# Cross attention: probabilities scaled by row before they are turned, and values as the stationary operand

## What is computed

```python
def memory_cross_attention(xn, memn, w_xq, w_xkv, w_xo):
    q = (xn @ w_xq).reshape(bsz, s, X_HEADS, X_HEAD_DIM)
    k, v = jnp.split(memn @ w_xkv, 2, axis=-1)
    scores = jnp.einsum("bshd,bmhd->bhsm", q, k) * (X_HEAD_DIM ** -0.5)
    p = jax.nn.softmax(scores, axis=-1)
    o = jnp.einsum("bhsm,bmhd->bshd", p, v).reshape(bsz, s, D_MODEL)
    return o @ w_xo
```

## Time and profile before

| what | value |
|---|---|
| median of 3 runs | 2702.12 us (2698.0 to 2704.2) |
| the profiled execution | 2703.93 us, its span 2702.2 us |
| mean granted TensorE clock | 0.984 |
| the attention block with the block of turns, from PE's first score to the first product with `w_xo`, layer 0 | 220.33 to 241.16 us |
| the same, layer 1 | 701.00 to 721.82 us |

### The profile page before, as it was taken

How to read it: one execution, slowest core, us unless ns; L and a number is a source line. 1 busy time by engine, 2 the same in 40 slices (tenths; PEclk the granted TensorE clock), 3 DMA queues, 4 the chain that set the end, 5 groups by cost and what they waited for, 6 DMA issues and landing times. The chain is left out here.

```text
span 2702.2 us, 79563 instructions
## 1 busy us (share of the span) xinstructions
PE 2553.2 (94%) x35795; PEld 2164.4 (80%) x35795; DVE 1013.4 (38%) x2465; ACT 446.6 (17%) x1027; POOL 162.0 (6%) x212
## 2 busy tenths in 40 slices
PE   8999999999979999999999999888999999999997
PEld 6888788788869989999989897666758678877775
DVE  4511444371120110110110101446673478765666
ACT  2101000110123322000000001410000445542000
POOL 0100000010012122000000000000000000001000
PEclk9999999999979999999999999999999999999999
DMA  7433454554459999999999997344553000010452
GB/s 226 158 125 125 156 163 140 152 171 141 191 192 407 407 408 405 374 407 407 408 407 407 407 406 219 118 135 155 174 192 125 3 7 7 7 67 22 158 176 104
DMA packets 289831, 571.33 MB, mean 211 GB/s; under 512 B 17622, under 2 KB 180436, under 8 KB 289700
## 3 DMA queue, kind: packets, MB, share of 16 engines
q1 hardware_dynamic: 289700, 569.49, 57.9%
HBM read 568.37 MB, written 5.28 MB: 212 GB/s over the span
## 5 line engine op out<-in xcount | busy, mean ns | idle before, releaser
L2226 PE MATMUL ps<-xg,ring 128*64 128x80 f32 x14336 | 512.1, 234 | 4.3 <-issue 1.1
L2226 PEld LDWEIGHTS ps<-xg,ring 128*64 128x64 f32 x14336 | 503.0, 138 | 11.6 <-DMA ring<-in_moe_w_up_dram 5.7
L2347 DVE TENSOR_TENSOR hidden<-acted,ps 128x320 f32<-128x320 f32 x64 | 28.6, 446 | 665.7 <-PE ps L2226 665.7
L2242 PE MATMUL ps<-hidden,expert_down 128*64 128x80 f32 x7168 | 259.6, 234 | 11.2 <-DMA expert_down<-in_moe_w_down_dram 4.5
L2242 PEld LDWEIGHTS ps<-hidden,expert_down 128*64 128x64 f32 x7168 | 253.0, 138 | 15.5 <-issue 9.3
L622 PE MATMUL ps<-xT,ring 128*128 128x256 f32 (+1 forms) x944 | 215.9, 390 | 11.7 <-PEq L600 4.5
L622 PEld LDWEIGHTS ps<-xT,ring 128*128 128x128 f32 (+1 forms) x944 | 178.0, 190 | 46.7 <-issue 12.6
L622 PE MATMUL ps<-ring,xT 128*128 128x256 f32 (+1 forms) x928 | 192.7, 369 | 4.7 <-PEq L1298 2.0
L622 PEld LDWEIGHTS ps<-ring,xT 128*128 128x128 f32 x928 | 168.6, 190 | 28.3 <-issue 7.1
L401 POOL TENSOR_SCALAR stat<-stat 128x1 f32<-128x1 f32 x30 | 13.6, 454 | 1697.7 <-ACT junk L396 1255.3
L1674 PEld LDWEIGHTS ps<-xT,ring 128*128 128x128 f32 x720 | 88.5, 195 | 27.1 <-issue 18.7
(11 more groups left out here) (465 smaller groups left out, 3669.8 us busy)
## 6 DMA issues: line engine op xcount, KB each, us to landing
expert_down<-in_moe_w_down_dram SPq DMA_DIRECT2D x96, 1024.0 KB, 16.9
ring<-in_moe_w_gate_dram SPq DMA_DIRECT2D x84, 896.0 KB, 16.1
ring<-in_moe_w_up_dram SPq DMA_DIRECT2D x84, 896.0 KB, 16.6
ring<-in_mlp_w_dram SPq DMA_DIRECT2D x64, 1024.0 KB, 5.6
second<-in_moe_w_gate_dram SPq DMA_DIRECT2D x22, 1792.0 KB, 15.4
second<-in_moe_w_up_dram SPq DMA_DIRECT2D x22, 1792.0 KB, 16.0
ring<-in_w_xkv_dram SPq DMA_DIRECT2D x16, 1024.0 KB, 5.4
expert_down<-in_moe_w_down_dram SPq DMA_DIRECT2D x32, 512.0 KB, 16.4
```

What stands on the lines that cost most here:

```text
L2226: mm = pe.matmul(bank[b][o:o + HEAD, at, :], w[:, c, f * P + o:f * P + o + HEAD], xg[:, p * E_STEP + c, :], start=(p == 0 and c == 0 and a ...
L2242: mm = pe.matmul(yT[c // 4][o:o + HEAD, c % 4, :], w[:, j, c * P + o:c * P + o + HEAD], hidden[:, f, :], start=False, stop=False, skip_gro ...
L2347: dve.tensor_tensor(hidden[:, part, :], acted[:, part, :], src, ALU.mult).then_inc(hidden_ready, 1)
```

## The change

`attend` takes the turned tensor `oT` instead of `o_rows`. The reciprocal and the scaling become `normalize(h)`, which scales the probabilities in place, row by row, before the turn; `turn(h)` waits for it instead of for the exponentials. The value matmuls take a 128-column part of the values as the stationary operand and the turned probabilities as the moving one, so that the output of head h comes out turned, in two parts of 128x256, which DVE copies into `xT`. `turn_only` and its call go.

```diff
-    def attend(self, heads, o_rows, scale, qT, kT, v, ahead):
+    def attend(self, heads, oT, scale, qT, kT, v, ahead):
...
-            op = [[ps[:, 4 + 2 * b + t, 0:dh] for t in range(TT)] for b in range(2)]
+            parts = v(0, 0).shape[1] // P
+            op = [[ps[:, 4 + 2 * b + c, 0:SEQ] for c in range(parts)] for b in range(2)]
...
                     def turn(h):
-                        pe.wait_ge(probs.sem, probs.at(per_tile * (h + 1)))
+                        pe.wait_ge(normed.sem, normed.at(h + 1))
...
-                        for t in range(TT):
+                        for c in range(parts):
                             for m in range(TT):
-                                mm = pe.matmul(op[h % 2][t], pT[:, h % 2, m, t * P:(t + 1) * P], v(h, m), start=(m == 0), stop=(m == TT - 1))
+                                mm = pe.matmul(op[h % 2][c], v(h, m)[:, c * P:(c + 1) * P], pT[:, h % 2, m, :], start=(m == 0), stop=(m == TT - 1))
                         mm.then_inc(o_done.sem, 1)
...
+                    def normalize(h):
+                        dve.wait_ge(probs.sem, probs.at(per_tile * (h + 1)))
+                        chain.link(dve.reciprocal(rden[:, h, :], den[:, h, :]))
+                        for t in range(TT):
+                            last = dve.tensor_scalar(p_sb[:, h % 2, t, :], p_sb[:, h % 2, t, :], rden[:, h, t:t + 1], None, ALU.mult)
+                        last.then_inc(normed.sem, 1)
+
                     maximum(0)
                     maximum(1)
+                    normalize(0)
                     for h in range(heads):
                         if h + 2 < heads:
                             maximum(h + 2)
-                        dve.wait_ge(probs.sem, probs.at(per_tile * (h + 1)))
-                        chain.link(dve.reciprocal(rden[:, h, :], den[:, h, :]))
+                        if h + 1 < heads:
+                            normalize(h + 1)
                         dve.wait_ge(o_done.sem, o_done.at(h + 1))
-                        for t in range(TT):
-                            last = dve.tensor_scalar(o_rows[:, t, h * dh:(h + 1) * dh], op[h % 2][t], rden[:, h, t:t + 1], None, ALU.mult)
+                        for c in range(parts):
+                            last = dve.tensor_copy(oT[:, parts * h + c, :], op[h % 2][c])
                         last.then_inc(o_stored.sem, 1)
...
-    def turn_only(self, rows, dst, loads=None):
...
-            o = self.spare_rows
-            self.attend(XH, o, XD ** -0.5,
+            self.attend(XH, self.xT, XD ** -0.5,
...
-            self.turn_only(o, self.xT)
         self.add_rows(self.xT, 256, self.h)
```

More of the change, by code:

```diff
@@ L1043, in attend @@
             tp = [ps[:, 2 + b, :].rearrange("p (t m) -> p t m", t=TT) for b in range(2)]
-            dh = v(0, 0).shape[1]
-            op = [[ps[:, 4 + 2 * b + t, 0:dh] for t in range(TT)] for b in range(2)]
-            scores, mxr, probs, turned, pT_ready, o_done, o_stored = (
-                self.scores_done, self.max_ready, self.probs_ready, self.probs_turned, self.probsT_ready, self.heads_done, self.head_stored)
+            parts = v(0, 0).shape[1] // P
+            op = [[ps[:, 4 + 2 * b + c, 0:SEQ] for c in range(parts)] for b in range(2)]
+            scores, mxr, probs, normed, turned, pT_ready, o_done, o_stored = (
+                self.scores_done, self.max_ready, self.probs_ready, self.sig("probs_normed"), self.probs_turned, self.probsT_ready, self.heads_done, self.head_stored)
             chain = Chain(self.nc.vector, self.vec_step)
@@ L1129, in _ @@
                             maximum(h + 2)
-                        dve.wait_ge(probs.sem, probs.at(per_tile * (h + 1)))
-                        chain.link(dve.reciprocal(rden[:, h, :], den[:, h, :]))
+                        if h + 1 < heads:
+                            normalize(h + 1)
                         dve.wait_ge(o_done.sem, o_done.at(h + 1))
-                        for t in range(TT):
-                            last = dve.tensor_scalar(o_rows[:, t, h * dh:(h + 1) * dh], op[h % 2][t], rden[:, h, t:t + 1], None, ALU.mult)
+                        for c in range(parts):
+                            last = dve.tensor_copy(oT[:, parts * h + c, :], op[h % 2][c])
                         last.then_inc(o_stored.sem, 1)
             self.vec_step.over(chain.n)
+            normed.over(heads)
             for s, n in ((scores, heads), (mxr, heads), (probs, per_tile * heads), (turned, heads), (pT_ready, heads), (o_done, heads), (o_stored, heads)):
```

## The result

The changed kernel takes **2710.36 us** in the median of 8 runs (2704.14 to 2714.89) against 2700.45 of the kernel before in 8 runs (2697.65 to 2705.03): a ratio of **1.0034**, 95% interval 1.0022 to 1.0046. It is slower, by 9.9 us in the median, and the interval puts that at some 6 to 12 us. The profiled execution has a span of 2711.3 us, 9.1 more than before, at the same mean clock of 0.984.

A forecast was written before the change was run, and what follows sets the result against it. PE, busy 94% of the span, was taken as the bound; 1.39+1.87+1.93+1.84-0.12-2.92 gave +3.99 us a layer, +8.0 for two, 2711.9 for the profiled execution and 2710 for a median, range 2704 to 2719.

The forecast's parts named there:

- the signs that the text had named: PE idle 1.65 to 1.75 us before each turn, turn(3) 14.0 after turn(0), products 4.0 and 8.0 later, clock 1.00.
- turn(0): First turn on PE in layer 0: waits for the scaling, at 225.73 instead of 224.34, +1.39 us.
- From turn to turn: PE, layer 0: spacings 4.09, 5.82 and 4.05 us instead of 2.22, 3.89 and 2.21: +1.87, +1.93, +1.84.
- The block of turns: Before the products with w_xo: removing 16 transposes, their copies and one block boundary gives -2.92 us a layer.
- The store of values: DVE, end of the block: two copies out of PSUM span 0.76 us where two scalings spanned 0.88, -0.12 us.
- the end from turn(3) to the products: Layer 0: turn(3) at 239.69, block end at 244.76, PE going on 0.39 later at 245.15 instead of 241.16.
- The scaling is hidden: Rival: turns find the probabilities already scaled, so the saved block counts; 6.1 us won, 2696; chance 0.06.
- the point from which it decides: Where normalize(h+1) ends against score(h+2): ahead of max(2) the scaling could be done by 226.9, before 228.1.
- The clock falls: Rival: PE's clock falls in the new holes, 1.7 us lost a fall; 2713 to 2717, or 2724; chance 0.17.
- The expert stage absorbs the delay: Rival: expert loads keep their times, so only layer 0 pays; 2706; chance 0.10.
- The edits at no cost: Value matmuls with operands swapped: eight instructions span 1.89 us either way, taken as 0.
- SP in layer 1 was covered: SP's last issue would end at 719.4, inside the block ending at 725.4; next limit if the block got 2 us shorter.

The follow-up runs named there:

- Experiment 1: The changed kernel with normalize(h+1) ahead of maximum(h+2) on DVE, all work the same; ratio 0.9995 to the kernel before, median 2701.55 us.
- experiment 3: The changed kernel with PE's scores one head earlier and DVE's order adapted, all work the same; ratio 0.9987 to the kernel before, median 2699.86 us.
- experiment 2: The changed kernel without scaling the probabilities, turns waiting for the exponentials again; ratio 0.9983 to the kernel before, median 2697.28 us.
- experiment 4: The kernel with scores one head earlier, plus layer 1's last expert-weight load issued one block later; ratio 0.9980 to the kernel before, median 2696.28 us.

## Why the prediction was right, and where it wasn't

**The forecast** was 2710, and the median is 2710.36; the ratio of 1.0034 stands against the +0.30% of the text. The mechanism is the one that was named: the scaling stands behind a maximum, or behind copies, that wait for PE. Experiment 1 shows it for the two middle holes by moving the scaling ahead of the maximum alone, experiment 3 for all four by putting other work of PE between each scaling and its turn. Of the signs that the text had named, the holes came out at 1.57 to 1.71 us (1.65 to 1.75), turn(3) 13.86 us after turn(0) (14.0), and the products of layer 1 6.94 us later (8.0).

**Term by term**, layer 0: turn(0) came 5.39 us after the first score, where it was 224.34-220.33 = 4.01 before: +1.38 (1.39 forecast). From turn to turn it is 4.09, 5.82 and 3.95 (4.09, 5.82 and 4.05), so +1.87, +1.93 and +1.74. The block of turns gave back its 2.92, for the products begin 0.39 us behind DVE's last copy (244.32), as PE went on 0.39 behind DVE before. Two terms were a little off. The store of values starts 0.04 us behind the matmuls, not the 0.12 taken from the row at 229.00, which shortens the round of turn(3). For the same reason, and because the last two value groups span 3.62 us (3.72 before; why isn't shown), the end from turn(3) to the products took 5.29 where 5.46 was forecast (239.69 to 245.15). Sum: +3.71 a layer instead of +3.99, **+7.44** in all instead of 8.0.

**The rest of the 9.1 us of the two spans** isn't part of the change. Where PE's last feed-forward begins, the changed kernel is 7.06 us behind (2481.95 against 2474.89); that stage then takes 213.9 us instead of 211.9. In experiments 1 to 4 it took 212.9, 214.2, 214.5 and 214.3, so the profile of before has the shortest of the six. PE waits in it for DVE's tile `made` for 1.0 us before and 2.4 in the changed kernel; what holds DVE up stays open.

A second stage whose instructions are the same moves as well: from the norm that opens layer 1 to its first score it took 204.7, 204.4, 201.8, 204.4, 201.9 and 204.4 us in the profiles of before, the changed kernel and experiments 1 to 4. That goes with the clock. The stage has two holes, of 2.89 and 2.23 us, which are the same within 0.01 us in all six. Before, in the changed kernel and in experiments 2 and 4 the clock falls to 1.2 GHz behind each of them (the earlier trace rows show the second); in experiments 1 and 3, the two short ones, it stays at 2.4 GHz. The 128 products behind the second hole span 29.56 us before (670.66 to 700.22) and 27.86 in experiment 1, whose timeline and one of its windows are these:

```profile
669.47 27.86 PE L622 MATMUL ps<-xT,ring 128*128 128x256 f32 x128 [2.23 <-PEq L600]
```

```profile
671.50:672.50 1.00, 1.00 (x6) 0.90 (x5) 0.00 (x0) 0.00 (x0) 0.00 (x0) 1.00 0.18 55
```

So two single spans differ by a few microseconds without a cause in the change. That the median meets the forecast to 0.4 us is partly luck: the kernel before came out 1.7 us lower in 8 runs than in the 3 that the forecast started from, the medians lie 9.9 apart where 8.0 was forecast, and the blocks give 7.44. The last lies inside the interval of 6 to 12; the blocks' own stretches, which repeat to 0.1 us, are what the sum should be judged by.

**The rivals.** *The scaling is hidden* is refuted for the order in the diff, and the point from which it decides was right: with normalize ahead of the maximum the two middle holes go. But the text's 2696 for that case needed all four to go. Turn(0) has no score to hide behind in that order, and normalize(3) still stands behind the copies, so experiment 1 came out at before's time; it took experiments 3 and 4 to reach 2696. *The clock falls* didn't happen in the profiled execution, with holes of 1.57 to 1.71 us, but it was near: behind the eight holes of 1.97 to 2.10 us it fell once, behind the eight of 2.36 to 2.50 three times. Its price of 1.7 us a fall, taken from the earlier trace rows, was measured as 1.7 and 3.3 for one and two. *The expert stage absorbs the delay* is refuted: the products of layer 1 came 6.94 us later than in the earlier trace rows, the norm behind them 6.94 (757.47 against 750.53), and the first expert product 7.05 (789.10 against 782.05).

**The edits at no cost.** The value matmuls take 1.89 us a group with the values stationary, as with the operands the other way round. SP in layer 1 was covered, as forecast: its last issue, which waited for score(3), ended at 722.21, in a block that ran to about 728.4. That cover is gone in experiments 2 and 3, as the text had said of a shorter block; what the text hadn't priced is that the hole it leaves can bring the clock down as well.

## What to carry to other kernels

Work that moves from behind a product to ahead of it lands on the path between two engines, and here its cost was set less by its own length (0.87 us) than by what is queued ahead of it on its engine: a reduction that waits for the engine that is waiting. When a step of engine A needs engine B, write down both lists next to each other and give A something independent to do between the request and the use; scores made one head earlier turned +3.7 us a layer into -3.3 (in layer 1 only with the last issue moved as well). And a block that has become shorter must be looked at again for what ends it next, the DMA issues too.

## What the runs showed of the hardware

In layer 1 SP issues three loads of 1792 KB one behind the other at the end of its list. In experiments 2 and 3 these issues occupied it for 1.10, 4.66 and 4.76 us; in experiment 4 the third was issued 4.4 us after the second had gone out, and took 0.40. What SP waits for inside an issue isn't shown. At a block boundary that time counts like any other work.

The clock's answer to a hole of a given length isn't fixed. Four holes of 1.97 to 2.10 us left it at 2.4 GHz in one layer, and in the other it fell to 1.2 behind one of them; the holes of 2.23 and 2.89 us ahead of layer 1's scores were followed by falls in six of the eight profiles of this case, and by none in the other two. The holes of 1.57 to 1.71 us in the changed kernel's blocks never were, four in a row in either layer. That is no safe length, though: in the kernel before, in the second block, the clock fell behind a hole of 1.52 us, with one of 0.37 close ahead of it, while the same hole in the kernel with one extra scaling (at 1650.86) saw none. PE's timeline and a window of the kernel before:

```profile
1644.42 7.75 PE L622 MATMUL ps<-xT,ring 128*128 128x256 f32 x27 [1.52 <-PEq L456]
```

```profile
1645.00:1646.00 1.00, 1.00 (x4) 0.82 (x3) 0.00 (x0) 0.00 (x0) 0.00 (x0) 0.50 1.10 349
```

A fall lasted some 3.4 us by the windows and cost 1.5 to 1.7 us where PE was busy all through it. The Trainium skill ("TensorE: Matmul & The Clock Gate", section "A second HAM failure mode: psum-queue depth-cycling") tells of frequent short idling that makes the clock swing. The runs here show falls behind short holes, but not that they have to be frequent: one hole of 2.54 us was enough in experiment 3.
